# Five deferred weight splits on VectorE and a last stripe by token tile, in a two-layer DeltaNet and sparse-attention trunk

## The reference, cut to what matters

```python
h = x
h = h + gated_deltanet(rms_norm(h, g0), ...)      # 16 q/k heads, 32 v heads of 128, chunks of 64
h = h + swiglu_ffn(rms_norm(h, g1), ...)          # hidden width 5632
shared_kv = nsa_shared_kv(h, ...)
h = h + nsa_attention(rms_norm(h, g2), shared_kv, ...)
h = h + swiglu_ffn(rms_norm(h, g3), ...)
return rms_norm(h, final_norm_g)                  # h * rsqrt(mean(h*h) + 1e-6) * gain

# inside gated_deltanet, for each head and chunk:
l_mat = where(strict, (k*beta) @ k.T * decay, 0)
sol = triangular_solve(l_mat, [v*beta, k*beta*exp(g_cum)], lower, unit_diagonal)
v_new = u - w @ state
o = q_dec @ state + attn_qk @ v_new
state = state * exp(g_last) + k_dec.T @ v_new
```

## Time and profile before

| | |
|---|---|
| median of three runs | 2826.11 us |
| the profiled execution's own time | 2826.06 us |
| its span, first to last instruction | 2824.3 us |
| mean granted TensorE clock | 0.995 |
| TensorE busy | 2748.6 us (97%) |
| VectorE busy | 2219.1 us (79%) |
| ScalarE busy | 1648.8 us (58%) |
| GpSimd busy | 30.4 us (1%) |
| moved by DMA | 493.23 MB, mean 175 GB/s |

### The profile page before, as it was taken

The page is one execution under the profiler, slowest core; times in us unless marked ns, Lnnn a source line. Parts: engine busy times, 40 slices in busy tenths (PEclk is TensorE's granted clock), DMA queues, the critical chain, the costliest instruction groups (busy, mean ns, idle before and its releaser), DMA issues.

```text
span 2824.3 us, 40242 instructions
## 1 busy us (share of the span) xinstructions
PE 2748.6 (97%) x13456; PEld 2278.7 (81%) x13456; DVE 2219.1 (79%) x2721; ACT 1648.8 (58%) x2183; POOL 30.4 (1%) x29
## 2 busy tenths in 40 slices
PE   8999999999988999999999999999999999999998
PEld 6778887888866888888888888888888888888886
DVE  5867877878767778888888876557777888888887
ACT  6776767667665455555555555554455555555554
POOL 0000000000000000000000000000000000000000
PEclk9999999999999999999999999999999999999999
DMA  6534444445433466655565556643346665656564
GB/s 239 178 127 150 156 144 160 157 142 170 155 106 112 155 207 197 197 189 193 197 202 195 196 173 226 221 135 120 104 145 203 205 200 195 199 182 200 199 196 160
DMA packets 135096, 493.23 MB, mean 175 GB/s; under 512 B 15008, under 2 KB 15328, under 8 KB 134624
## 3 DMA queue, kind: packets, MB, share of 16 engines
q1 hardware_dynamic: 133776, 487.82, 52.2%
q10 hardware_dynamic: 1232, 4.23, 0.4%
HBM read 489.86 MB, written 2.13 MB: 174 GB/s over the span
## 4 chain that ended last, share of the span: by engine, by line
issue 54%; PE 40%; DVE 3%; ACT 2%; DMA 1%; POOL 0%; POOLq 0%; ACTq 0%; SPq 0%; DVEq 0%
PE ACC L729 7%; PE ACC L731 7%; PE ACC L730 7%; PE SIDE L939 4%; PE SIDE L941 4%; PE SIDE L940 4%; PE SIDE L737 1%; PE ACC L941 1%; PE ACC L939 1%; PE ACC L940 1%; DVE W_LO L1590 1%; DMA RAW<-stream 1%; PE SIDE L1115 1%; ACT W_HI L1171 1%; ACT WORK L1550 0%
## 5 line engine op out<-in xcount | busy, mean ns | idle before, releaser
L1590 DVE TENSOR_TENSOR W_LO<-RAW,W_HI 128x1024 fp32r<-128x1024 f32 x424 | 512.3, 1222 | 292.8 <-ACT W_HI L1171 289.8
L1171 ACT ACTIVATE W_HI<-RAW 128x1024 fp32r<-128x1024 f32 x424 | 442.7, 1057 | 217.2 <-PE ACC L731 185.3
L1409 ACT ACTIVATE W_HI<-WORK 128x1024 fp32r<-128x1024 f32 x320 | 327.3, 1033 | 346.1 <-PE SIDE L941 234.1
L729 PE MATMUL ACC<-W_HI,X_HI 128*128 128x512 f32 x1216 | 491.5, 404 | 16.0 <-DVE W_LO L1590 15.8
L731 PE MATMUL ACC<-W_HI,X_LO 128*128 128x512 f32 x1216 | 477.2, 392 | 0.0
L730 PE MATMUL ACC<-W_LO,X_HI 128*128 128x512 f32 x1216 | 477.0, 392 | 0.0
L1837 DVE TENSOR_TENSOR W_LO<-WORK,W_HI 128x1024 fp32r<-128x1024 f32 x300 | 364.0, 1219 | 124.2 <-ACT W_HI L1409 124.2
L1409 ACT ACTIVATE W_HI<-RAW 128x1024 fp32r<-128x1024 f32 x328 | 315.6, 979 | 239.2 <-PE ACC L731 137.0
L729 PE MATMUL ACC<-W_HI,A_HI 128*128 128x512 f32 x928 | 369.9, 399 | 0.7 <-issue 0.7
L731 PE MATMUL ACC<-W_HI,A_LO 128*128 128x512 f32 x928 | 362.5, 391 | 0.0
L730 PE MATMUL ACC<-W_LO,A_HI 128*128 128x512 f32 x928 | 362.0, 390 | 0.0
(11 more groups left out here) (353 smaller groups left out, 3795.5 us busy)
## 6 DMA issues: line engine op xcount, KB each, us to landing
RAW<-stream SPq DMA_DIRECT2D x752, 512.0 KB, 4.5
WORK<-stream SPq DMA_DIRECT2D x160, 512.0 KB, 4.7
WORK<-gdn_rows ACTq DMA_DIRECT2D x8, 512.0 KB, 5.5
WORK<-xt SPq DMA_DIRECT2D x4, 512.0 KB, 9.3
H<-x SPq DMA_DIRECT2D x2, 1024.0 KB, 13.6
out<-WORK SPq DMA_DIRECT2D x4, 512.0 KB, 3.9
WORK<-tails SPq DMA_DIRECT2D x2, 512.0 KB, 11.0
WORK<-gfin SPq DMA_DIRECT2D x1, 1024.0 KB, 6.7
```

What stands on the lines that cost most here:

```text
L729: nc.tensor.matmul(dst, hi[:, at:at + P], wh, start=first and h % 2 == 0 and q == 0, stop=False)
L1171: nc.scalar.activation(W_HI[:, h % WS, :], raw_piece(h), ACT.Copy).then_inc(hi_ready, 1)
L1409: nc.scalar.activation(dst, src, ACT.Copy).then_inc(hi_ready, 1)
L1590: nc.vector.tensor_tensor(W_LO[:, h % WS, :], raw_piece(h), W_HI[:, h % WS, :].bitcast(f32), SUB).then_inc(lo_ready, 1)
```

## The change

Two parts. First, in DeltaNet iterations 1 to 8, VectorE does not split the low part at the end of slots 1, 2, 4, 6 and 14, but after the steps of the following slot (`LO_HELD`). The same code is there for ScalarE's high parts with an empty list (`HI_HELD`), so that ScalarE's order stays.

Second, in the last stripe of the last feed-forward TensorE does all 12 matmuls of token tile 0 from both pieces and then the 12 of tile 1 (`last_products`). The addition, gain, squares, mean, power and scaling are done for each token tile by itself; columns are shared between VectorE and ScalarE, and the four stores go out tile 0 first.

```diff
+HI_HELD = ()
+LO_HELD = (1, 2, 4, 6, 14)
 
 def gdn_vector(dve, link, it):
+            held = None
             for hs in range(32):
...
                 for name, p, w_ in gdn_steps(it, hs):
                     gdn_step_vector(dve, link, name, p, it - 1 if w_ == SOLVE else it, it)
-                if part:
+                if held is not None:
+                    split_lo(dve, c, held)
+                held = h + WS if part and hs in LO_HELD and not first and not last else None
+                if part and held is None:
                     split_lo(dve, c, h + WS)
 
+        def last_products(pe, c):
+            for t in range(NT):
+                dst = ACC[1][:, t * COLS:(t + 1) * COLS]
+                for h in (30, 31):
+                    if t == 0:
+                        pe.wait_ge(lo_ready, c + (h + 1))
+                    for q in range(2):
+                        at = (2 * (h % 2) + q) * SEQ + t * P
+                        wh, wl = (b[:, h % WS, q * COLS:(q + 1) * COLS] for b in (W_HI, W_LO))
+                        m = three(dst, B_HI[:, at:at + P], B_LO[:, at:at + P], wh, wl, h == 30 and q == 0, h == 31 and q == 1)
+                    if t:
+                        m.then_inc(w_used, 1)
+                if t == 0:
+                    m.then_inc(t0_done, 1)
 
 # ScalarE, after the last stripe
-                stripe_squares(act, ph, 3)
-                act.wait_ge(rstd, 5)
-                for half in range(2):
-                    part = hn[:, 1, half * 1024:(half + 1) * 1024]
-                    nc.scalar.activation(part, part, ACT.Copy, scale=rstd_c[:, 1:2]).then_inc(y_act, 1)
+                square(0)
+                scaled(0, 0)
+                square(1)
+                scaled(0, 1)
+                scaled(1, 3)
 
 # VectorE, after the last stripe
-                dve.wait_ge(sumsq, 16)
-                link(nc.vector.reduce_sum(sumsq_c, fin_parts.rearrange("p (t k) -> p t k", k=4), axis=AX.X))
...
+                last_stripe(0)
+                mean(0)
+                last_stripe(1)
+                scale(0, 2 * COLS, COLS)
+                mean(1)
+                scale(0, 3 * COLS, COLS)
+                scale(1, 0, 2 * COLS)
+                scale(1, 2 * COLS, COLS)
 
 # SyncE
-            for half in range(2):
+            for t, half, by_act, by_dve in ((0, 0, 2, 0), (0, 1, 0, 2), (1, 0, 0, 3), (1, 1, 3, 4)):
                 cols = slice(half * 1024, (half + 1) * 1024)
...
+                if by_act:
+                    sp.wait_ge(y_act, by_act)
+                if by_dve:
+                    sp.wait_ge(y_dve, by_dve)
+                sp.dma_start(out[t * P:(t + 1) * P, cols], hn[:, t, cols]).then_inc(out_done, 16)
 
 # GpSimd
-            pool.wait_ge(fin_mean, 1)
-            nc.gpsimd.tensor_tensor(rstd_c, sumsq_c, minus_half[:, 0:2], ALU.pow).then_inc(rstd, 1)
+            for t in range(NT):
+                pool.wait_ge(fin_mean, t + 1)
+                nc.gpsimd.tensor_tensor(rstd_c[:, t:t + 1], sumsq_c[:, t:t + 1], minus_half[:, t:t + 1],
+                                        ALU.pow).then_inc(rstd, 1)
```

More of the change, by code:

```diff
@@ L638, in build @@
          att_done, fin_mean, y_dve, y_act, out_done, dve_chain, pool_chain,
-         t_done, m1_out, mix, silu_f, hid_done, z_step, z_hi, z_lo, act_lo, cmp_out) = (sem(n) for n in (
+         t_done, m1_out, mix, silu_f, hid_done, z_step, z_hi, z_lo, act_lo, cmp_out, t0_done, h_t0) = (sem(n) for n in (
              "in_head in_const in_masks sm_zero x_first tail_in w2_in fin_in pad_zero hi_ready lo_ready w_used x_hi sumsq rstd tail_hi tail_lo "
@@ L644, in build @@
              "att_done fin_mean y_dve y_act out_done dve_chain pool_chain "
-             "t_done m1_out mix silu_f hid_done z_step z_hi z_lo act_lo cmp_out").split())
+             "t_done m1_out mix silu_f hid_done z_step z_hi z_lo act_lo cmp_out t0_done h_t0").split())
         x_in = [sem(f"x_in{i}") for i in range(NT)]
@@ L998, in ffn_tensor @@
                     turn(by_block(hid), 0)
+                if final_ and not nxt and k == 3:
+                    last_products(pe, c)
+                    continue
                 for half in range(2):
@@ L1381, in gdn_scalar @@
                     gdn_step_scalar(act, name, p, it - 1 if w_ == SOLVE else it, it, a_free)
-                if part:
+                if held is not None:
+                    split_hi(act, c, held)
+                held = h + WS if part and hs in HI_HELD and not first and not last else None
+                if part and held is None:
                     split_hi(act, c, h + WS)
@@ L1480, in ffn_scalar, with square, scaled @@
             else:
-                stripe_squares(act, ph, 3)
-                act.wait_ge(rstd, 5)
-                for half in range(2):
-                    part = hn[:, 1, half * 1024:(half + 1) * 1024]
-                    nc.scalar.activation(part, part, ACT.Copy, scale=rstd_c[:, 1:2]).then_inc(y_act, 1)
+                def square(t):
+                    act.wait_ge(*((acc_out[1], ph.after("down3", FBLK)) if t else (h_t0, 1)))
+                    nc.scalar.activation(fin_junk[:, (6 + t) * COLS:(7 + t) * COLS], H[:, t, 3 * COLS:4 * COLS], ACT.Square,
+                                         accum_out=fin_parts[:, 4 * t + 3:4 * t + 4]).then_inc(sumsq, 1)
+                def scaled(t, k):
+                    act.wait_ge(rstd, 5 + t)
+                    part = hn[:, t, k * COLS:(k + 1) * COLS]
+                    nc.scalar.activation(part, part, ACT.Copy, scale=rstd_c[:, t:t + 1]).then_inc(y_act, 1)
+                square(0)
[3 more added lines that the diff above has]
+                scaled(1, 3)
         def kv_scalar(act):
@@ L1948, in ffn_vector @@
                     e = 24 + 2 * k + half
-                    if half == 1:
+                    if half == 1 and not (final_ and not nxt and k == 3):
                         add_to_h(dve, c + (26 + 2 * k), k % 2, k)
@@ L1958, in ffn_vector @@
                     norm_vector(dve, nxt[0], nxt[1], k - 1, nxt[2])
-                if final_ and not nxt:
+                if final_ and not nxt and k < 3:
                     if k == 0:
@@ L1970, in ffn_vector, with last_stripe, mean, scale @@
             else:
-                link(i)
-                dve.wait_ge(sumsq, 16)
-                link(nc.vector.reduce_sum(sumsq_c, fin_parts.rearrange("p (t k) -> p t k", k=4), axis=AX.X))
-                nc.vector.tensor_scalar(sumsq_c, sumsq_c, 1.0 / DM, EPS, MUL, ADD).then_inc(fin_mean, 1)
-                dve.wait_ge(rstd, 5)
-                for half in range(2):
-                    part = hn[:, 0, half * 1024:(half + 1) * 1024]
-                    nc.vector.tensor_scalar(part, part, rstd_c[:, 0:1], None, MUL).then_inc(y_dve, 1)
+                def last_stripe(t):
+                    dve.wait_ge(*((w_used, c + 32) if t else (t0_done, 1)))
+                    part, scaled = H[:, t, 3 * COLS:4 * COLS], hn[:, t, 3 * COLS:4 * COLS]
+                    nc.vector.tensor_tensor(part, part, ACC[1][:, t * COLS:(t + 1) * COLS],
+                                            ADD).then_inc(*((acc_out[1], 1) if t else (h_t0, 1)))
+                    dve.wait_ge(*((acc_out[1], ph.after("down3", FBLK)) if t else (h_t0, 1)))
+                    link(nc.vector.tensor_tensor(scaled, part, gfs[:, 3 * COLS:4 * COLS], MUL))
+                def mean(t):
+                    dve.wait_ge(sumsq, 15 + t)
+                    link(nc.vector.reduce_sum(sumsq_c[:, t:t + 1], fin_parts[:, 4 * t:4 * t + 4], axis=AX.X))
+                    nc.vector.tensor_scalar(sumsq_c[:, t:t + 1], sumsq_c[:, t:t + 1], 1.0 / DM, EPS, MUL,
+                                            ADD).then_inc(fin_mean, 1)
+                def scale(t, at, n):
+                    dve.wait_ge(rstd, 5 + t)
+                    part = hn[:, t, at:at + n]
+                    nc.vector.tensor_scalar(part, part, rstd_c[:, t:t + 1], None, MUL).then_inc(y_dve, 1)
+                last_stripe(0)
[6 more added lines that the diff above has]
+                scale(1, 2 * COLS, COLS)
         def blocks_vector(dve, kv, half):
```

## The result

The changed kernel takes 2808.57 us (median of four runs, 2805.42 to 2810.22) against 2827.05 us of the kernel before (four runs): ratio 0.9937, 95% interval 0.9925 to 0.9949. Of the 18.5, 0.9 is a fourth run of the kernel before, which moved its median from 2826.11. The profiled execution takes 2808.15 us, span 2806.4 us, 17.9 less than the profiled one before. Two more sets of runs, on chips 11 and 1, gave 0.9935 and 0.9933.

What follows compares the result with a forecast made beforehand. TensorE, busy 97% of the span, and its waits were taken as the bound. Holds 10.8 us (5.5 + 2.0 + 1.2 + 2.1) and the end 2.4 made 13.2 off 2826.06, so 2812.9 us; range 2806 to 2824.

Steps and rivals of the forecast that it cites:

- rival 1: TensorE's clock loss in iteration 8 goes too with the shorter waits, 3.4 us more, 2809.5 us; chance 0.20.
- The wait at t3 and its origin on VectorE in slot 7: TensorE waits 1.11 us at t3 of slot 11 for ScalarE's late copy, since VectorE's low parts delay t2 and u2.
- The narrow place at piece 10: Slot 6's held low part, behind t2, u2 and dif, is ready only 0.4 us before TensorE wants it; costed at nothing.
- Rival 3: Slower: TensorE waits for the held low parts, 2.7 us in five iterations, 13.5 less 2.4, giving 2837.2 us; chance 0.06.
- Gain per body iteration 1.11: The t3 wait goes in each of five body iterations, 5.5 us in all; bounds 0 and 1.11 each.
- "Nothing in the body" for slot 14: Holding slot 14 makes u4 early, but ScalarE's stripe copy stands before its UR copies, so no gain in body iterations.
- Iteration 8: u2 about 1.1 us earlier shortens t3's wait, and 1.0 at t4: 2.1 us (0 to 5.0).
- t2's early start: In slot 6, t2 starts when its product is there, 331.15 instead of 333.45; it covers piece 10's later low part.
- The end: Tile-by-tile finish of the last feed-forward: first store 2.6 us earlier, last 1.8; taken as 2.4 us.
- The steps written for the fourth store: Square's sum, mean, power, scaling and issues after TensorE's end: fourth store at 2817.2 instead of 2819.00, 1.8 us earlier.
- The clock, left at nothing: TensorE's half-speed loss in iteration 8, 3.4 us, entered the sum as nothing, from -3.4 to +3.4.
- Rivals 2 and 4: Waits only move elsewhere, or the hold takes no effect; only the end gains 2.4: 2823.7 us; chance 0.14 together.

## Why the prediction was right, point by point

- **Ahead or behind.** Faster by 0.2% and more had 0.80; the sign, the places and the wide range (2806 to 2824) hold. 2808.57 lies 0.4 us below the forecast's own range (2809 to 2818), and nearer to rival 1's 2809.5 than to 2812.9, though not by rival 1's way. The profiled pair is 17.9 us apart where the sum had 13.2: it was a quarter short. By stages, measured against forecast: iteration 1 1.9 for 1.0; the five body iterations 7.7 for 5.5; iteration 7 3.3 for 2.2; its tail a loss of 1.6 for 0; iteration 8 2.85 for 2.1; the attention 1.1 for 0; the end 2.7 for 2.4. That the tail and the attention nearly cancel is luck.
- **The wait at t3 and its origin on VectorE in slot 7: right.** It is gone in iterations 1 to 7, with the 1.0 us of reserve that was worked out, and t2 starts when its product is there, 2.3 us earlier within its iteration, as forecast.
- **The narrow place at piece 10: right.** 0.45 us to spare against 0.4. Two runs made it too narrow, and the wait for W_LO came in slot 10 both times, if smaller (0.54 for 0.8, 0.49 for 0.7). Rival 3 is therefore a true mechanism, with its deciding point where the prediction put it, and it costs 0.8 us per iteration there; its price of 13.5 us was not seen.
- **"Gain per body iteration 1.11": mis-sized, the term of the sum that fell short most.** It is 1.53, in five iterations 7.6 us instead of 5.5. At t3 alone it is 1.28. The idle time of a row counts from the modelled end of the matmul before, 0.39 us after its start, while unbroken matmuls start every 0.23 us: a wait of TensorE between such matmuls costs those 0.17 too. The other 0.25 are at y2 (0.06), nw (0.12) and others too small to show as waits. In iteration 1 likewise 1.9 us came for 1.0: t4, t5 and nw each 0.2 earlier, with no wait shown in front of the first two. (The prediction opens with most of what can be had lying in iterations 1, 7 and 8. The body, with 7.7 us, gave as much as they did.)
- **"Nothing in the body" for slot 14: nearly.** 0.07 us per iteration at nw. In iteration 7 the part from t4 to nw is 1.75 us shorter than before, of which 1.38 are slot 14's hold, where 1.2 were taken, and t5 waits for nothing: right.
- **Iteration 8: right by the chain, 1.25 and 1.46 us for 1.1 and 1.0, wrong in what would show it.** I wrote that t4 would wait under 0.3 us; it waits 1.26. In the kernel before a stretch at half speed lies right behind t3; in this profile it is gone, so TensorE arrives at t4 earlier and waits as long. The changed kernel's second and third profiles settle it: both have a half-speed stretch between t3 and t4, t4 waits for nothing, as I had forecast, and t3 to t4 takes 8.15 us, only 0.16 more than without it. From the second:

```profile
872.60:876.00 3.40, 3.40 (x9) 2.53 (x8) 3.35 (x6) 1.67 (x3) 0.00 (x0) 0.50 0.60 205
...
879.32 0.60 PE L807 MATMUL SIDE<-YB,UB 128*64 128x64 f32 x8
```

Likewise t1 to t3 takes 17.3 us in ten of the eleven profiles of kernels that hold slots 1, 2 and 4 (17.65 in the other), and 18.56 in the three that do not hold them, with half-speed stretches in some of either kind. So in this iteration the solve's chain sets the time and nearly hides a half-speed stretch.
- **Which hold does it: not asked, and the steps of the sum suggest the wrong one.** The prediction gave t2's early start to slot 6. The runs show that slots 1, 2 and 4 suffice for the body, and that with slot 6 alone more than half of the gain at t3 is lost again at piece 10.
- **The end: right.** First store 2.12 us behind the last matmul (2.1 worked out), end of span 2.7 us earlier for 2.4; the stream's start decides, and the stores follow it. I had taken less than the first store's 2.6 for caution. (The steps written for the fourth store add up to 2815.5 where 2815.7 stands; nothing in the sum rests on it.)
- **The clock, left at nothing: right for this pair, by cancelling; rival 1 half right.** The profiled run before has five stretches at half speed ahead of its end, the three of the change three, four and five. In this pair both that lay in iteration 8 are gone (granted 1.00 there instead of 0.96), as rival 1 had it, but its 3.4 us did not come with them, since the chain hides them; in the tail of iteration 7 there is one more. Over all runs there are somewhat fewer: the granted clock averages 0.9953 in 46 runs of the kernel before, 0.9962 in 11 with the new end alone, and 0.9968 in 14 of the change. The last step, 0.0006 of 2810 us, is 1.7 us of full clock, the size of one such stretch (the row above has 3.5 us granted 0.52): as an estimate, one fewer by the holds. The step before it holds the new end too, where TensorE has stopped. What it adds to the 18.5 us, at most 1.6, no run here separates. By the rule of the Trainium skill (TensorE: Matmul & The Clock Gate, "What's actually happening") activity releases the throttle; the trace agrees as far as each stretch in these profiles, ahead of the end, begins during a wait of TensorE or within 3 us behind one, the shortest of these 1.48 us. But a wait does not tell it: the 2.14 us of ru bring one in two iterations and none in three, and the 3.22 us at t3 of iteration 8 none in this profile and one in the change's other two.
- **Rivals 2 and 4 (waits moved, 2823.7): out** by the run with the end alone, 2822.28, which leaves 14 us to the holds, and by the one with the holds alone.

## What to carry to other kernels

Where engines run fixed lists, look for a filler (here the split of a weight piece, with three slots to spare) that stands in front of a link of a dependency chain, above all one that itself waits for another engine; put the link first, and count how much spare time each filler has, since the delays add up over consecutive slots. Judge a hold together with those before it: alone it may only move the wait. And when a step is moved to another slot, look at what stands in front of its successor on every engine: one held low part was the difference between some 10 us lost and 2 to 3 us won.

## What the runs showed of the hardware that was not expected

- A wait of TensorE costs more than its row shows: 1.11 shown and 1.28 measured at t3, 0.49 shown and 0.77 measured at piece 10, in both cases the same in each body iteration.
- A stretch at half speed can cost almost nothing: between t3 and t4 of iteration 8, where TensorE else waits 1.26 us, it costs 0.15 to 0.4 us in the eight profiles that have slot 6's hold and a stretch there (8.14 to 8.38 us instead of 7.99), against some 1.4 to 1.6 us in full work.
- One kernel's profiled runs repeat the body iteration to 0.03 us (111.05, 111.03, 111.05, the last two on different chips), while some half-speed stretches outside it are in one profile and not in another. Over 46 runs of the kernel before, the 10 with a mean granted clock of 0.997 average 2824.3 us and the 13 with 0.994 average 2827.7: the clock goes with about half of the variance of the time between runs of one kernel; what the rest is stays open.
